# Cross attention's sample V: split in two fp32r parts, or moved unsplit in fp32 over four strips of PSUM

## What is computed

```python
def mem_kv(mem, norm_g, w_kv):
    k, v = jnp.split(rmsnorm(mem, norm_g) @ w_kv, 2, axis=-1)
    return (k.reshape(bsz, MEM_LEN, X_HEADS, X_HEAD_DIM), v.reshape(...))

def cross_attn(h, k, v, w_q, w_o):
    q = (h @ w_q).reshape(bsz, l, X_HEADS, X_HEAD_DIM)
    s = jnp.einsum('blhd,bmhd->bhlm', q, k) * (X_HEAD_DIM ** -0.5)
    p = jax.nn.softmax(s, axis=-1)
    o = jnp.einsum('bhlm,bmhd->blhd', p, v).reshape(bsz, l, D_MODEL)
    return o @ w_o
```

## Time and profile before

| | |
|---|---|
| median of 3 runs | 1935.46 us (1933.3 to 1940.47) |
| span of the profiled execution | 1942.3 us |
| TensorE, matmuls busy | 1807.2 us (93%), 13440 records |
| VectorE busy | 1295.6 us (67%) |
| ScalarE busy | 876.9 us (45%) |
| GpSimd busy | 211.9 us (11%) |
| HBM read, written | 320.95 MB, 38.66 MB: 185 GB/s over the span |

### The profile page before, as it was taken

The page is one execution under the profiler, slowest core; times in us unless marked ns, Lnnn a source line. Parts: engine busy times, 40 slices in busy tenths (PEclk is TensorE's granted clock), DMA queues, the critical chain, the costliest instruction groups (busy, mean ns, idle before and its releaser), DMA issues.

```text
span 1942.3 us, 34244 instructions
## 1 busy us (share of the span) xinstructions
PE 1807.2 (93%) x13440; PEld 1654.0 (85%) x13440; DVE 1295.6 (67%) x2257; ACT 876.9 (45%) x1172; POOL 211.9 (11%) x305
## 2 busy tenths in 40 slices
PE   7999898998979899988899999999898898899998
PEld 7999898997765555987799999999886687789998
DVE  5765678785886766468766656665656668757653
ACT  5433455464666644342443434333434542544433
POOL 1001101100110010201120011001311121120001
PEclk9999999999999999999999999999999999999999
DMA  8656644444895698657556657665734468536653
GB/s 222 181 167 178 204 120 137 149 128 133 258 280 167 218 298 264 207 195 260 196 146 179 171 171 199 175 179 164 239 93 142 149 243 289 197 109 173 182 162 113
DMA packets 463585, 361.01 MB, mean 186 GB/s; under 512 B 14633, under 2 KB 435781, under 8 KB 463429
## 3 DMA queue, kind: packets, MB, share of 16 engines
q1 hardware_dynamic: 409904, 254.87, 45.0%
q0 software_dynamic: 20288, 71.94, 10.8%
q10 hardware_dynamic: 33280, 32.65, 4.9%
HBM read 320.95 MB, written 38.66 MB: 185 GB/s over the span
## 4 chain that ended last, share of the span: by engine, by line
PE 67%; DVE 12%; ACT 11%; issue 5%; DMA 3%; ACTq 0%; POOL 0%; SPq 0%; DVEq 0%; POOLq 0%
PE psum L263 18%; PE psum L264 18%; PE psum L265 18%; ACT whi L211 4%; DVE wlo L217 4%; DMA raw<-in_w_xkv 2%; PE psum L1723 2%; ACT hb L1503 1%; PE psum L826 1%; PE psum L480 1%; PE psum L591 1%; DVE vl L2190 1%; PE psum L1350 1%; PE psum L2215 1%; DVE sb L1745 1%
## 5 line engine op out<-in xcount | busy, mean ns | idle before, releaser
L217 DVE TENSOR_TENSOR wlo<-raw,whi 128x2048 fp32r<-128x2048 f32 (+2 forms) x261 | 553.4, 2120 | 284.3 <-ACT whi L211 283.7
L263 PE MATMUL psum<-xnh,whi 128*128 128x264 f32 x2328 | 676.3, 290 | 5.7 <-DVE ht L1169 4.3
L264 PE MATMUL psum<-xnl,whi 128*128 128x264 f32 x2328 | 665.7, 286 | 0.0
L265 PE MATMUL psum<-xnh,wlo 128*128 128x264 f32 x2328 | 664.9, 286 | 0.0
L211 ACT ACTIVATE whi<-raw 128x2048 fp32r<-128x2048 f32 (+2 forms) x261 | 460.9, 1767 | 132.9 <-DMA raw<-in_w_xkv 60.1
L263 PEld LDWEIGHTS psum<-xnh,whi 128*128 128x128 f32 x2328 | 444.8, 191 | 24.6 <-issue 23.5
L264 PEld LDWEIGHTS psum<-xnl,whi 128*128 128x128 f32 x2328 | 445.2, 191 | 0.3
L265 PEld LDWEIGHTS psum<-xnh,wlo 128*128 128x128 f32 x2328 | 442.6, 190 | 0.0
L263 PE MATMUL psum<-Hh,whi 128*128 128x264 f32 x704 | 200.9, 285 | 0.0
L265 PE MATMUL psum<-Hh,wlo 128*128 128x264 f32 x704 | 200.0, 284 | 0.0
L264 PE MATMUL psum<-Hl,whi 128*128 128x264 f32 x704 | 199.1, 283 | 0.0
(11 more groups left out here) (563 smaller groups left out, 3080.3 us busy)
## 6 DMA issues: line engine op xcount, KB each, us to landing
raw<-in_w_ffn_in SPq DMA_DIRECT2D x176, 512.0 KB, 5.0
raw<-in_w_in_ab SPq DMA_DIRECT2D x88, 512.0 KB, 4.7
raw<-in_w_ffn_out SPq DMA_DIRECT2D x64, 384.0 KB, 4.0
raw<-in_w_ffn_out SPq DMA_DIRECT2D x64, 320.0 KB, 3.4
sb<-in_state_ret POOLq DMA_DIRECT2D x32, 512.0 KB, 6.3
out<-sb ACTq DMA_DIRECT2D x32, 512.0 KB, 3.6
raw<-in_w_out_ab SPq DMA_DIRECT2D x32, 512.0 KB, 5.2
kc<-in_cache_mem_k POOLq DMA_DIRECT2D x32, 512.0 KB, 7.1
```

What stands on the lines that cost most here:

```text
L217: nc.vector.tensor_tensor(wlo[:, c % SLOTS, 0:m], raw[:, c % SLOTS, 0:m], whi[:, c % SLOTS, 0:m].bitcast(F32), ALU.subtract).then_inc(lo_d ...
L263: e.matmul(out, a, hi[:, kk, 0:S.cols], start=first, stop=False)
L264: e.matmul(out, a, lo[:, kk, 0:S.cols], start=False, stop=False)
L265: m = e.matmul(out, b, hi[:, kk, 0:S.cols], start=False, stop=final)
```

## The change

- `SplitValues`, `vh` and `vl` are gone. `pm` is plain fp32 with 8 columns a token and is half as large.
- `SampleValues` does one fp32 matmul for each half of the memory and each head, 8 a token, straight on `vc`. Head h writes to partitions 32h to 32h + 7 of bank 4, columns 0 to 255.
- `MaskProbs` comes behind `Divide(0)` on VectorE; it first waits for the prompt's last exponential and sets partitions 0 to 103 of bank 4 to zero, then makes one copy in place of two operations.
- `vc` has three buffers of two tokens (the first lies where `xnh` is, as `vh` did). Tokens 0 and 1 are loaded by `FirstV` behind the third chunk of the K projection, 2 and 3 by the new `NextV` behind the fourth, 4 and 5 by `LaterV`, where 2 and 3 were; `SampleValues` of tokens 0 and 1 issues 6 and 7.
- `SampleRows` copies 104 x 256; `SampleOut` picks a head's 8 rows with a slice of the identity.
- Tokens 0 to 4 lie under LV; behind it the order is token 5, Values(0), token 6, Values(1), token 7, SampleRows, Values(2), SampleOut, Values(3).

```diff
-                vc=[place(f"vc{i}", [P, 2, 2, D], at=R + at) for i, at in enumerate((0, 82304))],
-                vl=[place(f"vl{i}", [P, 2, 2, D], F32R, at=R + at) for i, at in enumerate((0, 82304))],
-                vh=place("vh", [P, 2, 2, D], F32R, at=xn_at))
+                vc=[place(f"vc{i}", [P, 2, 2, D], at=at) for i, at in enumerate((xn_at, R, R + 82304))])
...
             class FirstV(Stage):
+                def pool(S, e):
+                    q_out(e)
+                    for b in range(2):
+                        load_v(e, b)
+
+            class NextV(Stage):
                 def pool(S, e):
                     mem_split(e)
-                    for b in range(2):
+                    for b in (2, 3):
                         load_v(e, b)
...
-                   mid={1: [units[1]], 2: [units[3]], 3: [units[5]]}, hooks={0: [q_rows, units[0]], 1: [units[2]], 2: [units[4]], 3: [FirstV(), units[6]]})
+                   mid={1: [units[1]], 2: [units[3]], 3: [units[5]]}, hooks={0: [q_rows, units[0]], 1: [units[2]], 2: [FirstV(), units[4]], 3: [NextV(), units[6]]})
...
                 def dve(S, e):
+                    e.wait_ge(X["exp"], 8 * lc + 8)
+                    e.memset(psum[0:104, 4, 0:256], 0.0)
                     ps_ready(e)
                     e.wait_ge(X["pm"], 2 * lc + 1)
                     src = B.pTs[:, :].rearrange("p (m b h) -> p m h b", m=2, b=NS)
-                    hi, lo = [B.pm[:, :, c:128:17].rearrange("p (m h) b -> p m h b", m=2) for c in (0, 8)]
-                    link(e, "dve", e.tensor_copy(hi, src))
-                    e.tensor_tensor(lo, src, hi.bitcast(F32), ALU.subtract).then_inc(X["pm"], 1)
+                    e.tensor_copy(B.pm[:, :, 0:64:9].rearrange("p (m h) b -> p m h b", m=2), src).then_inc(X["pm"], 1)
...
-            class SplitValues(Stage):
...
-                    nc.scalar.activation(B.vh[:, b % 2, :, :], B.vc[b // 2 % 2][:, b % 2, :, :], ACT.Copy).then_inc(X["qh"], 1)
...
                     for m_ in range(2):
                         for h in range(XH):
-                            o, c = psum[0:16, 4 + h // 2, (h % 2) * XD:(h % 2 + 1) * XD], slice(h * XD, (h + 1) * XD)
-                            p = B.pm[:, m_ * XH + h, b * 16:b * 16 + 16]
-                            e.matmul(o, p, B.vh[:, b % 2, m_, c], start=b == 0 and m_ == 0 and h % 2 == 0, stop=False)
-                            m = e.matmul(o, p, B.vl[b // 2 % 2][:, b % 2, m_, c], start=False, stop=b == NS - 1 and m_ == 1 and h % 2 == 1)
+                            m = e.matmul(psum[32 * h:32 * h + NS, 4, 0:XD], B.pm[:, m_ * XH + h, b * NS:(b + 1) * NS], B.vc[b // 2 % 3][:, b % 2, m_, h * XD:(h + 1) * XD],
+                                         start=b == 0 and m_ == 0, stop=b == NS - 1 and m_ == 1)
                     m.then_inc(X["spv"], 1)
...
                     for t in range(KD):
-                        m = e.matmul(psum[:, 5, t * NS:(t + 1) * NS], B.ost[:, t // 4, (t % 4) * P:(t % 4 + 1) * P], sum2, start=True, stop=True)
+                        h = t // 2
+                        m = e.matmul(psum[:, 5, t * NS:(t + 1) * NS], B.ost[0:104, (t % 2) * P:(t % 2 + 1) * P], ident[0:104, 32 * h:32 * h + NS], start=True, stop=True)
...
-                        mid={0: [units[7]], 1: [SampleSoftmax()] + k_turn + [SP_[0]], 2: [MaskProbs(), SP_[1], Divide(0), SV[0]],
-                             3: [SV[2], SP_[3], Divide(2)] + p_turns[0]},
-                        hooks={0: [SC[0]] + score_turn + [LaterV(), SC[1]], 1: prob_turn + [SC[2], SC[3]], 2: [SV[1], SP_[2]],
-                               3: [SV[3], SP_[4]] + p_turns[1]})
+                        mid={0: [units[7]], 1: [SampleSoftmax()] + k_turn, 2: [Divide(0), MaskProbs(), SV[0]],
+                             3: [SV[2], Divide(2)] + p_turns[0]},
+                        hooks={0: [SC[0]] + score_turn + [LaterV(), SC[1]], 1: prob_turn + [SC[2], SC[3]], 2: [SV[1]],
+                               3: [SV[3], SV[4]] + p_turns[1]})
...
-            stages.extend([Values(0), SV[4], SP_[5], Values(1), SV[5], SP_[6], Values(2), SV[6], SP_[7], Values(3), SV[7], SampleRows(), SampleOut()])
+            stages.extend([SV[5], Values(0), SV[6], Values(1), SV[7], SampleRows(), Values(2), SampleOut(), Values(3)])
```

More of the change, by code:

```diff
@@ L1994, in build @@
         X = {n: sem_of("x_" + n) for n in ("mem_in", "score", "nmax", "exp", "prob", "pv", "oh", "ol", "qb", "kused", "smax", "sexp", "sprob",
-                                           "spv", "soh", "sol", "qh", "ql", "pm", "ost", "spo")}
+                                           "spv", "soh", "sol", "pm", "ost", "spo")}
         KR = 8
         kc_in = [sem_of(f"kc_in{i}") for i in range(KR)]
-        vc_in = [sem_of(f"vc_in{i}") for i in range(4)]
+        vc_in = [sem_of(f"vc_in{i}") for i in range(6)]
         xbuf = None
@@ L2009, in cross_buffers @@
                 pp=place("pp", [P, 8, MEM], at=tab_at), pT=place("pT", [P, XH, 512], at=R + 57344),
-                qr=place("qr", [40, 1024], F32R, at=R + 65792), pm=place("pm", [P, 8, 128], F32R, at=R + 69888),
-                ost=place("ost", [16, 2, 512], at=R + 73984), sc=place("sc", [P, 2, 32], at=R + 78080),
+                qr=place("qr", [40, 1024], F32R, at=R + 65792), pm=place("pm", [P, 8, 64], at=R + 69888),
+                ost=place("ost", [P, XD], at=R + 73984), sc=place("sc", [P, 2, 32], at=R + 78080),
                 ps_=place("ps_", [32, MEM], at=R + 78336), pTs=place("pTs", [P, 64], at=R + 79360),
@@ L2063, in load_v @@
                 for m_ in range(2):
-                    e.dma_start(B.vc[b // 2 % 2][:, b % 2, m_, :],
-                                A["cache_mem_v"][layer, b, m_ * P:(m_ + 1) * P].rearrange("p h d -> p (h d)")).then_inc(vc_in[b % 4], 16)
+                    e.dma_start(B.vc[b // 2 % 3][:, b % 2, m_, :],
+                                A["cache_mem_v"][layer, b, m_ * P:(m_ + 1) * P].rearrange("p h d -> p (h d)")).then_inc(vc_in[b % 6], 16)
             mem_turn = behind(lambda: Turn([([(B.mtok[:, q % 2, (k + q // 2) * P:(k + q // 2 + 1) * P], P, P, q * P) for q in range(4)],
@@ L2155, in pool @@
                         e.wait_ge(X["sol"], lc)
-                    e.memset(B.pm[:, :, :].bitcast(F32), 0.0).then_inc(X["pm"], 1)
+                    e.memset(B.pm[:, :, :], 0.0).then_inc(X["pm"], 1)
                 def dve(S, e):
+                    e.wait_ge(X["exp"], 8 * lc + 8)
+                    e.memset(psum[0:104, 4, 0:256], 0.0)
                     ps_ready(e)
@@ L2170, in pool @@
                     e.wait_ge(X["kused"], 2 * NS * lc + 12)
-                    for b in (2, 3):
+                    for b in (4, 5):
                         load_v(e, b)
-            class SplitValues(Stage):
[L2177 to L2184, removed]
-                    nc.scalar.activation(B.vh[:, b % 2, :, :], B.vc[b // 2 % 2][:, b % 2, :, :], ACT.Copy).then_inc(X["qh"], 1)
[L2187 to L2191, removed]
             class SampleValues(Stage):
@@ L2321, in dve @@
                         e.tensor_tensor(B.ol[:, i, 0:NP], psum[:, 6 + i % 2, 0:NP], B.oh[:, i, 0:NP].bitcast(F32), ALU.subtract).then_inc(X["ol"], 1)
-            SV, SP_, SC = [SampleValues(b) for b in range(NS)], [SplitValues(b) for b in range(NS)], [Scores(h) for h in range(XH)]
+            SV, SC = [SampleValues(b) for b in range(NS)], [Scores(h) for h in range(XH)]
             LV = Linear(W, 4, KD, 2, by_cols(W, D), (B.mh, B.ml), dve=v_out, cols=256, turned=True, early=True, late=True,
-                        mid={0: [units[7]], 1: [SampleSoftmax()] + k_turn + [SP_[0]], 2: [MaskProbs(), SP_[1], Divide(0), SV[0]],
-                             3: [SV[2], SP_[3], Divide(2)] + p_turns[0]},
-                        hooks={0: [SC[0]] + score_turn + [LaterV(), SC[1]], 1: prob_turn + [SC[2], SC[3]], 2: [SV[1], SP_[2]],
-                               3: [SV[3], SP_[4]] + p_turns[1]})
+                        mid={0: [units[7]], 1: [SampleSoftmax()] + k_turn, 2: [Divide(0), MaskProbs(), SV[0]],
+                             3: [SV[2], Divide(2)] + p_turns[0]},
+                        hooks={0: [SC[0]] + score_turn + [LaterV(), SC[1]], 1: prob_turn + [SC[2], SC[3]], 2: [SV[1]],
+                               3: [SV[3], SV[4]] + p_turns[1]})
             kv_out = evicted()
```

9 lines of the change are left out of this document (4 added, 5 removed).

## The result

On one chip, beside the kernel before (1937.27 us), the changed kernel takes 1905.52 us (1898.7 to 1910.6). The ratio is 0.9827, 95% interval 0.9802 to 0.9853: about 32 us less. The profiled executions have spans of 1942.3 and 1906.1 us. The forecast was 1907.5.

The account below looks back on a forecast made before the run. TensorE, busy for 93% of the span, was taken as the bound. Layer 0 -13.5 and layer 1 -13.3, with 1.2 us for the clock, gave -28 us off the median 1935.5: 1907.5 us, eight-in-ten range 1899 to 1929.

Parts of the forecast that it names:

- TensorE's work on the sample's V: Cross attention: eight tokens of unsplit fp32 on four strips take 9.5 us a layer in place of 15.0, 5.5 less.
- the second rival: Only two of four strips overlap: token 1.73 us, 1920.5 us, chance 0.15; skill-page estimate for four: 1.09 us, time 1910.
- Going over to strips and back: Switching TensorE to the strips' matmuls and back costs 0.3 us a block, seven blocks a layer: 2.1 us.
- The score chain: Second score stages: without vh and vl ahead of the weight chunk's split, wlo ends 2.1 us sooner a layer.
- The first token: Token 0 waits some 0.5 us more, MaskProbs standing behind Divide with a PSUM memset taken at 0.4 us.
- The tail: Last transposes to output projection: new order hides waits, 6.4 us less in layer 0, 6.2 in layer 1.
- The clock: TensorE's clock, halved after idle times, gives back 1.2 us in tail, score chain and projection; bounds 0 and 6.
- DMA: 2 MB of V loads move into the full stretch 886 to 914; the next weight chunk's delay costed at nothing.
- a rival of 10 us: Full DMA engines delay the chunk of V's second projection: 2 x 5 = 10 us, 1917.5 us; chance 0.10.
- Series in one bank: Heads writing to one PSUM bank go in series: a token 3.46 us, 1948 us in all; chance 0.14.
- only two of the four strips overlap: In the sample's V matmuls a token takes 1.73 us, 13 us more in all, 1920.5 us; chance 0.15.

Follow-up runs that it names:

- e1: Changed kernel with all four heads of the sample's V on one strip (partitions 0 to 7), still unsplit fp32: 1945.47 us, ratio 1.0032 to the kernel before.
- e2: Changed kernel with two strips in place of four (partitions 0 and 32, banks 4 and 5): 1923.6 us, ratio 0.9915 to the kernel before.
- e3: Changed kernel plus value-preserving passes of each token's V through ScalarE and VectorE, about where the splits stood: 1938.55 us, ratio 0.9993 to the kernel before.
- e9: Changed kernel with the passes of e3, moved a token or so sooner under LV: 1938.84 us, ratio 1.0020 to the kernel before.
- a0: The changed kernel run again, nothing edited: 1904.96 us, ratio 0.9814 to the kernel before.
- e5: Changed kernel with SSDHeads taking its heads in the order 0, 1, 2, 3 in place of 0, 2, 1, 3: 1906.09 us, ratio 0.9844 to the kernel before.

## Why the prediction was right, step by step

**TensorE's work on the sample's V.** Predicted 9.5 us a layer. On the kernel after's chain seven blocks take 7.8 us and each follower some 0.2 more than the usual 0.12: 9.1. Of the bounds for a token the lower one, 0.87, was the right one (two in a row take 1.84), and the 1.09 of the second rival's estimate was too high; e1 (+41.6 us over both stretches, 41 by the prediction's 3.46 a token) and e2 (14.6 for 13) show that the price between the bounds goes by the number of strips. Four strips get through the token 3.6 times as fast as one (3.55 against 0.98). Going over to strips and back costs 0.2 to 0.3 a block, as read from the earlier trace rows.

**The score chain.** Predicted 2.1 less. From ScalarE's freedom to the reduction it was 918.78 to 925.12, 6.3 us. In the kernel after, the chain of waits:

```profile
921.37 1.81 ACT whi L211
...
923.20 2.29 DVE wlo L217
925.49 0.35 DVE st L2250
```

4.1 us, 2.2 less.

**The first token.** Predicted 0.5 more, with a memset of 0.4. The memset of 104 x 256 takes 0.27 us (timeline of VectorE):

```profile
931.23 0.27 DVE L2168 MEMSET psum<- 104x256 f32 x1
```

TensorE's token 0 starts at 931.68, 0.22 behind what it could have; the step was right, its size a little high.

**The tail.** From the end of the last transposes to the projection, token 4 counted in both: 23.7 before; after 13.2 + 0.98 = 14.2. The prediction's terms give 23.7 - 6.4 for the waits, less 4 x 0.94 for the tokens and some 1.1 more for their blocks: 14.6. The last wait is 0.98, where 1.1 was said for the eviction of Values(3). Layer 0 adds up as -2.2, -9.5 and -2.7 for the middle: -14.4 (predicted -13.5).

The size is right, but not whose waits they were. The prediction names `vh` and `vl` ahead of tokens 5 to 7 first. They are long on the chain, yet TensorE worked on another token and another block of Values meanwhile. Its own waits before, 921.6 to 972.4 (us in total, times, longest):

```profile
PE psum L2257 <- ACT pp L2269: 2.6, 1, 2.6
PE psum L2309 <- issue: 2.1, 1, 2.1
PE psum L2229 <- DVE ost L2222: 1.3, 1, 1.3
PE psum L2215 <- DVE vl L2190: 1.0, 3, 0.6
```

The first is the score chain (0.4 in the kernel after, so again 2.2 less). In the tail the three tokens waited only 1.0 us for `vl` (2.0 in layer 1). Values(0) waited 2.1 for the eviction of the transposes, SampleOut 1.3 for the copy, the projection 0.6 for SampleOut's eviction: 4.0 us that the new order of the stages covers but for the last 0.98, in both layers. So some 3 us a layer of the gain belong to the order, and the split's own part is the 2.2 of the score chain and these 1.0 or 2.0. No run has the order alone, so this rests on the traces. Of the 7.5 us that the prediction called waits and slow clock these waits are 5.0 in layer 0. Most of the rest is the clock: a mean of 0.57 from 951.9 to 955.8, 1 us behind the end of the wait of 2.1; in the kernel after there is no such stretch.

**The clock.** Mis-sized, within its bounds of 0 to 6: I took 1.2 us. Layer 1 gained 15.6 where 13.3 was said, and its stretch ran at 0.95 before and 1.00 after. And the clock came back behind the stretch. Windows of the first 20 us of the projection, layers 0 and 1, before, then after:

```profile
972.40:992.40 20.00, 19.97 (x152) 19.97 (x153) 10.56 (x9) 6.98 (x7) 5.04 (x4) 0.92 0.38 106
1711.10:1731.10 20.00, 19.93 (x145) 19.93 (x146) 9.68 (x8) 7.02 (x7) 5.03 (x4) 0.87 0.38 106
```

```profile
960.60:980.60 20.00, 20.00 (x165) 20.00 (x166) 12.10 (x10) 8.22 (x10) 6.48 (x6) 1.00 0.42 115
1677.60:1697.60 20.00, 19.96 (x165) 19.99 (x166) 12.07 (x10) 8.22 (x10) 6.44 (x6) 1.00 0.42 115
```

TensorE is fully busy in all four and gets through 152 and 145 matmuls before and 165 after. At 0.92 and 0.87 that is 1.6 and 2.6 us lost. The loss lies at the start, as the first 3.6 us of layer 0's projection show, in the kernel before:

```profile
972.40:976.00 3.60, 3.57 (x17) 3.57 (x18) 2.05 (x1) 1.52 (x1) 0.00 (x0) 0.54 0.00 0
```

In the last 4 us ahead of it TensorE had worked for only 2 us, between waits of 1.3 and 0.6; in the kernel after it has one wait, of 0.98, behind more than 12 us of unbroken work. From the second projection to the end it was 231.2 us before and is 228.5 in the kernel after and in every experiment. That holds for e3 and e9 too: in layer 0 their stretches at half clock end 12 us ahead of the projection (966.6 and 957.6), and their last wait but the 0.98 (1.5 and 1.7 us) ends 7.5 us ahead of it. So this part is shown in size for the last projection, 2.7 us; that the waits just ahead bring the cut clock on is how the rows read, and no run tests it. Between the first projection and layer 1's query rows the profile before has 632.6 us, the one after 627.3 and a0 629.9; 1.6 of it is the clock above, the rest is not explained and no larger than the scatter of this part in the other runs (624.6 to 630.7).

**DMA.** Costed at nothing, with a rival of 10 us. The experiment with later loads points at 2 us and leaves room for some 5, so the size of 10 falls and a smaller loss stays open.

**The other rivals.** Series in one bank falls by the four starts within 0.02 us, and by e2 and e5. That only two of the four strips overlap falls by the halving from e2 to the changed kernel. What the prediction didn't see is e3: it booked the strips' own saving at 11 us and the waits at 17, as if each stood by itself. In the change's order neither half alone gives a gain: strips with the passes 0.9993, no passes without strips 1.0032, both 0.9827. The terms added up for the edit as a whole; they don't say what a part of it is worth.

## What to carry to other kernels

The fp32 matmuls here, with 8 columns of weights, cost by the number of 32-partition strips that they are spread over (3.55, 1.83 and 0.98 us a token). So an fp32 operand that would be split on ScalarE and VectorE may be left whole if four outputs can lie on four strips. Read an engine's idle time from its own waits, not from the others' pieces on the chain: in the tail before, `vh` and `vl` of a token hold 4.2 us of the chain twice, and TensorE stood idle for 0.2 and 0.8 us meanwhile. Look first whether TensorE is what the stage waits for: in three more places (SSDHeads, retention, the matrix memory) shorter work on TensorE did not move the time. And judge a stretch filled by DMA transfers from two executions of the same kernel, not from one.

## What the runs showed of the hardware

- Four fp32 matmuls of 8 columns of weights and 256 moving columns, on four column strips of one PSUM bank, start within 0.02 us of each other and run side by side: 16 records in 1.05 us, 1.90 on two strips, 3.62 on one.
- In SSDHeads the order of the heads decides whether their records overlap (1.50 us a block against 2.15), not the bank: the third head, with eight records of the other strip ahead of it, did not start beside the first.
- A memset of 104 x 256 in PSUM on VectorE takes 0.27 us, where I had estimated 0.4 from copies.
- In a stretch with a DMA share of 0.89 and 0.77 the same kernel took 48.7 and 57.0 us in two executions, the longer one at a granted clock of 0.91.
- At the granted clock of 0.50, behind 4.81 us of idle TensorE, a token on four strips took 1.89 us and a block of Values 3.73, where they take 0.98 and 1.92 at 1.00 (e3 and the kernel after).
